# SyncE issues the fourth expert's weights without waiting for the second expert's gathered rows

## What is computed

```
h = rmsnorm(x, g_mix);  u, q, k, v = split(h @ w_in)
x = x + concat(pool_mixer(u), diff_attention(q, k, v)) @ w_out
h2 = rmsnorm(x, g_ffn)
# router: best of 4 groups, then the best 2 of its 4 experts
for e in range(16):
    he  = silu(h2 @ w_gate[e]) * (h2 @ w_up[e])          # 1024 -> 256
    moe = moe + combine[..., e:e+1] * (he @ w_down[e])   # 256 -> 1024
y = rmsnorm(x + moe, g_final)
```

## Time and profile before

| | us |
|---|---|
| median of 3 runs | 452.24 (451.46 to 453.07) |
| profiled execution, its own time | 450.83 |
| profiled execution, span of the profile | 449.0 |
| TensorE busy | 421.5 (94%) |
| VectorE busy | 273.3 (61%) |
| ScalarE busy | 197.7 (44%) |
| GpSimd busy | 125.9 (28%) |
| mean granted TensorE clock | 0.975 of full speed |

### The profile page before, as it was taken

How to read it: one execution, slowest core, us unless ns; L and a number is a source line. 1 busy time by engine, 2 the same in 40 slices (tenths; PEclk the granted TensorE clock), 3 DMA queues, 4 the chain that set the end, 5 groups by cost and what they waited for, 6 DMA issues and landing times.

```text
span 449.0 us, 7775 instructions
## 1 busy us (share of the span) xinstructions
PE 421.5 (94%) x2927; PEld 366.0 (82%) x2927; DVE 273.3 (61%) x655; ACT 197.7 (44%) x485; POOL 125.9 (28%) x207
## 2 busy tenths in 40 slices
PE   7899999999999998999998999999999998999970
PEld 3786999997876866888895988999999997899950
DVE  3855232616778987364258796555577775497770
ACT  6475222505576664232124433344455554366340
POOL 2010000200242415251001304333335543466431
PEclk9999999999999999999998999999999999899995
DMA  7841605306000089613226599998899999963120
GB/s 268 302 160 47 223 1 182 111 1 195 1 1 2 1 334 364 261 52 149 89 93 244 178 403 392 379 361 352 354 360 355 344 369 352 349 231 120 55 81 21
DMA packets 32073, 91.36 MB, mean 203 GB/s; under 512 B 11200, under 2 KB 11712, under 8 KB 27942
## 3 DMA queue, kind: packets, MB, share of 16 engines
q1 hardware_dynamic: 20790, 71.97, 43.4%
q0 software_dynamic: 11248, 18.93, 12.0%
HBM read 86.38 MB, written 26.01 MB: 250 GB/s over the span
## 4 chain that ended last, share of the span: by engine, by line
PE 61%; issue 12%; DVE 7%; POOL 7%; DMA 6%; ACT 5%; POOLq 0%; SPq 0%; DVEq 0%; ACTq 0%
PE ps L1188 13%; PE ps L822 9%; PE ps L824 9%; PE ps L823 9%; DMA region_x<-h_rows,lists 5%; PE ps L1125 2%; PE ps L1181 2%; PE ps L1205 2%; PE ps L1206 2%; PE ps L1210 2%; PE ps L943 2%; PE ps L978 2%; POOL region_x L699 2%; DMA region_x<-in_x_prompt 1%; POOL mix L699 1%
## 5 line engine op out<-in xcount | busy, mean ns | idle before, releaser
L1188 PE MATMUL ps<-region_p,region_a 128*128 128x128 f32 x512 | 59.1, 276 | 0.6 <-DVE region_p L2025 0.6
L1188 PEld LDWEIGHTS ps<-region_p,region_a 128*128 128x128 f32 x512 | 57.9, 192 | 1.2 <-DVE region_p L2025 1.1
L824 PE MATMUL ps<-region_a_r,region_w_r 128*128 128x288 f32 x192 | 56.5, 294 | 0.0
L699 POOL DMA_INDIRECT region_x<-h_rows,lists x13 | 22.1, 1700 | 77.6 <-DVE slot_w L2123 77.6
L822 PE MATMUL ps<-region_a_r,ring_r 128*128 128x288 f32 x128 | 40.5, 317 | 0.0
L823 PE MATMUL ps<-region_a_r,ring_r 128*128 128x288 f32 x128 | 37.7, 295 | 0.0
L1575 ACT ACTIVATE region_p<-ps,gffn_sb 128x128 f32<-128x128 f32 x116 | 31.5, 382 | 10.9 <-PE ps L1181 10.9
L824 PEld LDWEIGHTS ps<-region_a_r,region_w_r 128*128 128x128 f32 x192 | 36.1, 188 | 0.0
L1596 ACT ACTIVATE region_t<-ps 128x256 f32<-128x256 f32 x16 | 6.1, 382 | 56.1 <-PE ps L1188 56.1
L1188 PE MATMUL ps<-region_p,ring 128*128 128x128 f32 x256 | 29.6, 277 | 0.6 <-DVE region_p L2047 0.4
L822 PEld LDWEIGHTS ps<-region_a_r,ring_r 128*128 128x128 f32 x128 | 24.0, 188 | 6.9 <-issue 3.3
(11 more groups left out here) (358 smaller groups left out, 1025.8 us busy)
## 6 DMA issues: line engine op xcount, KB each, us to landing
region_a<-in_w_gate SPq DMA_DIRECT2D x8, 1024.0 KB, 8.3
region_a<-in_w_up SPq DMA_DIRECT2D x8, 1024.0 KB, 13.2
region_a<-in_w_down SPq DMA_DIRECT2D x8, 1024.0 KB, 14.7
region_w<-in_w_in SPq DMA_DIRECT2D x2, 2048.0 KB, 10.2
region_w<-in_w_out SPq DMA_DIRECT2D x2, 2048.0 KB, 8.0
ring<-in_w_gate SPq DMA_DIRECT2D x4, 1024.0 KB, 9.2
ring<-in_w_up SPq DMA_DIRECT2D x4, 1024.0 KB, 13.9
ring<-in_w_down SPq DMA_DIRECT2D x4, 1024.0 KB, 13.1
```

The lines of the kernel that those rows point to most:

```text
L699: pool.indirect_dma_start(out=dst, out_offset=None, in_=src, in_offset=bass.IndirectOffsetOnAxis(ap=at, axis=0), bounds_check=bound[n], oo ...
L824: return pe.matmul(out, lhs_lo, rhs_hi, start=False, stop=last)
L1188: ins = pe.matmul(ps[:, 2 + b, (first + c) * P:(first + c + 1) * P], w[:, k, c * P:(c + 1) * P], xT[:, b, k, :], start=(k == 0), stop=(k = ...
```

## The change

SyncE no longer waits for the second expert's gathered rows before it issues the three loads of the fourth expert. Nothing else is changed, and the wait for the first expert's rows stays.

```diff
             sp.wait_ge(xg_loaded[0], 16)
             load_down(2, expert_at(2))
-            sp.wait_ge(xg_loaded[1], 16)
             load_expert(3, expert_at(3))
```

## The result

The changed kernel is faster. In 20 runs beside 20 of before its median is 450.25 us (447.46 to 459.16) against 452.88 us (450.67 to 455.73), a ratio of 0.9941 with a 95% interval of 0.9919 to 0.9964. By these three estimates the gain is 0.3 to 0.6%, 1.4 to 2.7 us. The run of 459.16 us counts as slow and is not in the ratio. The time lies inside the predicted range, but on the other side of before: +0.9 us was forecast.

What follows compares the result with a forecast made beforehand. The expert stage was taken as bound by TensorE, with DMA close behind. Terms +1.4 + 1.8 - 0.3 - 2.0 = +0.9 us on 452.24 gave 453.1 us, range 449.7 to 455.4 us.

Steps and rivals of the forecast that it cites:

- the two places: The second expert's gather, forecast to land late and cost time, and the late stall near 380 us, forecast to shorten.
- SyncE: Fourth expert's three loads issued 8.7 us sooner, the fifth expert's issue staying at 258.68 us; price 0.
- The second expert's gather, +1.4: Gather issued at 252.25 us meets weights, takes 8.3 us, lands at 260.55 us and delays TensorE by 1.4 us.
- The estimate of 7.55 us: Second expert's gather time if DMA engines alternate between queues: landing at 259.8 us, price 0.7 us instead of 1.4.
- my row: The fourth expert's gather, issued while weight loads were in flight, 8.3 us, taken for the second expert's gather.
- TensorE's clock, +1.8: A 1.9 us gap behind the second expert's late gather lowers TensorE's granted clock, costing 1.8 us.
- The next gathers, -0.3: Fourth expert's gather, costing TensorE 0.27 us at 280.62 us, should land in time: -0.3 us.
- The late stall, -2.0: Near 380 us, the 4.24 us loss shrinks by the 2.0 us DMA stood idle from 252 to 254 us.
- The range's lower end, 449.7 us: Whole-kernel time if the second expert's gather is in time and 2 us are won late.
- the sum it names: Rival with the second expert's gather in time: -0.3 - 2.0 = -2.3, 449.9 us; chance 0.24 including a late stall wholly gone.
- The reading of the dips as engines that never catch up: DMA share dips, as at 301 to 305 us, mean row-carrying engines stay busy, so time they win early is kept.

Runs made afterwards that it cites:

- these three estimates: Three sets of runs of the same changed kernel, each against the kernel before: ratios 0.9941, 0.9970 and 0.9965.
- less_up: Kernel before without loading seven eighths of the sixth expert's up weights (issued at 269 us); ratio to before 0.9995.
- less_up_8: Kernel before without loading seven eighths of the thirteenth expert's up weights (issued near 349 us); ratio to before 0.9948.
- split_gu: Kernel before with the fourth expert's gate and up weights issued without the wait, its down weights still behind it; ratio to before 0.9940.
- gate_only: Kernel before with only the fourth expert's gate weights issued without the wait, up and down still behind it; ratio to before 0.9975.
- split_again: Second set of the kernel before with the fourth expert's gate and up weights issued early, down weights behind the wait; ratio to before 0.9978.
- before_again: The kernel before, unedited, timed and profiled a second time; ratio to before 1.0023.
- gfin_late_b: Kernel before with the load of the final norm's gains (0.5 MB) issued three experts later; ratio to before 1.0028.
- after_up2: Kernel before with the fourth expert's weights held until the second expert's gate and up products end, about 12.4 us longer; ratio to before 1.0178.
- before_third: The kernel before, unedited, timed and profiled a third time; ratio to before 1.0011.
- no_waits_again: Second set of the changed kernel with the wait for the first expert's rows dropped too; ratio to before 0.9973.

## Why the prediction was wrong

It was right on the two places and on their signs. The sum came out on the wrong side because of the price put on TensorE's clock behind the late gather, and three other terms were off in size, one of them in sign too. The means of three profiles each of before and after are used.

1. *SyncE.* As forecast: three issues at 247 to 248.6 us, the next at 259.06 us.
2. *The second expert's gather, +1.4.* Right in kind. It took 260.00 - 252.62 = 7.4 us where 8.3 was taken, and from the first to the second expert's products it is 10.76 us instead of 10.26, +0.5 us (+0.9 and +0.6 in the other two profiles). In the other two profiles it took 7.8 and 7.5 us, the landing read from the start of its transposes. The estimate of 7.55 us, from what the Trainium skill says in "DMA: Bandwidth & Descriptors", section "Queues, rings and completion order", was nearer than my row, and the three landings lie near it. I had also misread rows 9: it wasn't for want of traffic that the first expert's gather landed in 5.2 us, since the DMA share is 0.91 in these 5.2 us. The true value lay between rows 9 and 10, and I took the upper end.
3. *TensorE's clock, +1.8.* **This step failed.** The gaps of 0.98 and 1.75 us were followed by transposes of 1.09 us, full speed, and neither of the other two profiles shows a slow one there. Measured 0 where 1.8 us were forecast: the granted clock stays at 1.00. The rows 13 and 14 on which it stood don't repeat. The same gap, 1.50 or 1.51 us, is there in all three profiles of before and all three of after, and only the first of before shows a lower clock behind it (0.62 from 178 to 182 us; 1.00 in the others). A fall behind such a gap is a chance, and I had priced it as certain.
4. *The next gathers, -0.3.* Wrong in sign. The fourth expert's gather took 9.8 us instead of 8.3 in the first profile; it cost 1.23 us of waiting on the mean of three (1.75, 0.82, 1.12), against 0.59 (0.27, 0.79, 0.70) before. Ahead of the third expert's products another 0.6 us is lost in all three (12.06 us instead of 11.45 us between products), twice in a wait for VectorE, once in one for that expert's gather. Together these places cost +1.25 us instead of -0.3. Why this gather takes longer though less is outstanding wasn't found; the load of the gains isn't the cause.
5. *The late stall, -2.0.* Right that it shortens, too small: the late number goes from 26.76 to 23.94 us, -2.8. Of this the waits are -1.65 us (3.23 to 1.58) and the clock about -1.1 us: it is low behind the late wait in two of three profiles of before, in none of after. So the clock did count, but at 380 us and as a gain.

Early +1.9 instead of +2.9, late -2.8 instead of -2.0: -0.9 instead of +0.9. Had the clock term been 0, the sum would have been -0.9, just what the profiles show; but that would have been luck, since the errors of the other three terms (-0.7, +1.5 and -0.8 us) cancel. The rest of the way to the timed gain, 1.4 to 2.7 us, the profiles don't explain: their sum from the first to the sixteenth expert's products is 172.91 us for before and 172.11 us for after, -0.8 us. The times say where it lies: the profiled executions of before took 450.83, 451.09 and 451.42 us, 1.3 us less on the mean than the medians of their sets (452.88, 452.74, 451.58), those of after 450.44, 450.64 and 450.21 us, within 0.2 us of theirs on the mean. So the profiles of before caught short executions, and most executions gain more than these profiles show. The range's lower end, 449.7 us, was also 0.2 us below the sum it names: 452.2 - 2.3 is 449.9 us.

The reading of the dips as engines that never catch up was too strict. Relief does decay, as less_up shows. That the late gain comes from weights moved out of the way is supported by less_up_8 and split_gu, more weakly by gate_only, and by the two sets of three profiles, and weakened by split_again and by less_up, whose relief of about the size of the change's at 380 us gave no gain. The last link is shown, late gathers that hold up VectorE's lists and with them the next gathers; how a lead won at 250 us reaches 350 us is argued, not shown.

## What to carry to other kernels

A transfer that is early by 15 us can still be worth issuing earlier: what counts is not only its own deadline but what still moves when other transfers are needed at once, here row gathers 130 us later. Look for microseconds of DMA share 0.00 ahead of a long stretch near 1, and price the delay of whatever small transfer lies in them against the late waits. Price a fall of the clock behind a gap as a chance, not from one gap in one profile, and don't read a difference of 1 us from one profile each.

## What the runs showed that I had not expected

TensorE's granted clock isn't foretold by the gap before it. Gaps of 2.43 and 2.52 us (before, split_again) were followed by eight transposes in 1.97 us, one of 2.06 us (before_again) by the same in 1.32 us; gaps of 2.24 and 2.33 us (gfin_late_b) and of 2.83 us (after_up2) by the same eight in 1.09 us, full speed.

```profile
403.52 1.09 PE L1181 MATMUL ps<-ident,region_x 128*128 128x128 f32 x8 [2.83 <-DMA region_x<-h_rows,lists]
```

From SyncE's first issue after the output projection (the first expert's down weights) to the first gate and up products it is 13.3 us in some profiles and 14.6 to 14.9 us in others, with no value between, in before (13.33, 13.33, 14.85) as in after (14.59, 13.25, 14.80). Here too it is the clock: in steps of 2 us from 240 to 248 us it is granted at 1.00, 0.62, 0.52 and 1.00 in before, at 0.62, 0.50, 0.50 and 0.68 in before_third. By the same estimate as above it costs 1.7 us there in the profiles with 13.3 us and 3.0 to 3.3 us in those with 14.6 us or more, except no_waits_again, which has 1.7 us and its wait of 1.25 us for the first gather. These 1.3 us lie ahead of the change's first effect and blur any comparison of two single spans.
